# The chunk recurrence of a hybrid decoder: four moves in the order of three engines' work

## The reference, cut to what matters

```
mLSTM (4 heads, 64 x 64):
  mt  = max(b + m, max over s<=t of (b_t - b_s + li_s));  w_inter = exp(b + m - mt)
  qk  = (q k^T) * exp(draw - mt)           num = w_inter * (q C) + qk v;  den likewise with n
  h   = num / max(|den|, exp(-mt))         C = w_c * C + ks^T v   (ks = k * exp(...))
gated DeltaNet (4 heads, 128 x 128):
  a   = strictly lower(beta * (k k^T) * gam);   solve (a + I) [w_v, w_k] = [v*beta, k*beta*exp(d)]
  u   = w_v - w_k S;   o = (q*exp(d)) S + ((q k^T)*gam) u;   S = exp(dl)*S + kdec^T u
HGRN2 (4 heads, 64 x 64):
  attn_ts = sum over channels of q_tc k_sc exp(bc_tc - bc_sc)
  o   = (q*exp(bc)) S + attn i;            S = exp(bl) * S + (k*exp(bl-bc))^T i
```

## Time and profile before

| | |
|---|---|
| median of 3 runs | 1974.97 us (1974.41 to 1976.78) |
| profiled execution | 1972.25 us, with a span of 1970.5 us |
| TensorE, share of the span | 1763.4 us, 89% |
| DVE, ACT, POOL | 913.5, 830.7 and 98.1 us |
| recurrence, first layer | 262 to 448 us, TensorE busy 149.03 us, mean granted clock 0.92 |
| recurrence, second layer | 1224 to 1406 us, TensorE busy 147.55 us, mean granted clock 0.94 |

### The profile page before, as it was taken

One profiled execution on the slowest core, in us unless ns is written; L12 is line 12 of the kernel. 1 busy time (PEld: TensorE's weight loads), 2 busy tenths in 40 slices (PEclk: granted clock), 3 DMA queues, 4 the chain that ended last, 5 costly groups with the idle time before them and its releaser, 6 DMA issues. The chain is left out here.

```text
span 1970.5 us, 35425 instructions
## 1 busy us (share of the span) xinstructions
PE 1763.4 (89%) x13446; PEld 1681.1 (85%) x13446; DVE 913.5 (46%) x1960; ACT 830.7 (42%) x1860; POOL 98.1 (5%) x165
## 2 busy tenths in 40 slices
PE   5999968878879999999889998788688799999995
PEld 5999957775679999999879997687658799999995
DVE  5275257756552222244363823666662522223354
ACT  5235555655243333333242355455542433333332
POOL 0020110003000000000002011000300000000000
PEclk8999999986789999999989999999669899999997
DMA  5322000003653323322042210000329223323211
GB/s 171 90 81 68 9 5 1 1 1 74 131 106 98 88 85 86 105 81 75 2 146 80 82 44 4 1 1 1 71 71 142 80 85 86 90 85 112 72 35 46
DMA packets 128706, 132.80 MB, mean 67 GB/s; under 512 B 32630, under 2 KB 95522, under 8 KB 128584
## 3 DMA queue, kind: packets, MB, share of 16 engines
q1 hardware_dynamic: 128584, 131.22, 25.1%
HBM read 121.53 MB, written 9.66 MB: 67 GB/s over the span
## 5 line engine op out<-in xcount | busy, mean ns | idle before, releaser
L307 PE MATMUL bank<-arena 128*128 128x272 f32 (+4 forms) x3488 | 1013.7, 291 | 32.2 <-DVE arena L414 14.7
L309 PE MATMUL bank<-arena 128*128 128x272 f32 (+4 forms) x3488 | 1011.0, 290 | 0.0
L308 PE MATMUL bank<-arena 128*128 128x272 f32 (+4 forms) x3488 | 1006.4, 289 | 0.0
L307 PEld LDWEIGHTS bank<-arena 128*128 128x128 f32 (+1 forms) x3488 | 655.2, 188 | 39.2 <-issue 25.3
L308 PEld LDWEIGHTS bank<-arena 128*128 128x128 f32 (+1 forms) x3488 | 656.2, 188 | 3.0 <-issue 2.1
L309 PEld LDWEIGHTS bank<-arena 128*128 128x128 f32 (+1 forms) x3488 | 655.8, 188 | 0.9
L351 DVE TENSOR_TENSOR arena<-sbuf,arena 128x512 fp32r<-128x512 f32 x296 | 201.2, 689 | 350.2 <-ACT arena L347 350.0
L347 ACT CAST arena<-sbuf 128x512 fp32r<-128x512 f32 x296 | 180.6, 622 | 352.2 <-PE bank L309 304.0
L2943 DVE TENSOR_TENSOR arena<-sbuf,arena 128x544 fp32r<-128x544 f32 x88 | 63.8, 724 | 143.2 <-ACT arena L2887 143.2
L2887 ACT CAST arena<-sbuf 128x544 fp32r<-128x544 f32 x88 | 56.9, 647 | 163.2 <-PE bank L309 160.0
L347 ACT CAST arena<-arena 128x512 fp32r<-128x512 f32 (+1 forms) x128 | 77.7, 622 | 112.7 <-PE bank L309 104.4
(11 more groups left out here) (374 smaller groups left out, 1794.0 us busy)
## 6 DMA issues: line engine op xcount, KB each, us to landing
sbuf<-in_w_gate_up SPq DMA_DIRECT2D x176, 256.0 KB, 3.1
arena<-in_w_in SPq DMA_DIRECT2D x96, 256.0 KB, 2.8
sbuf<-in_w_down SPq DMA_DIRECT2D x88, 256.0 KB, 2.6
arena<-in_w_in SPq DMA_DIRECT2D x32, 260.0 KB, 2.6
sbuf<-in_w_out SPq DMA_DIRECT2D x32, 256.0 KB, 4.8
sbuf<-in_state_gdn_S SPq DMA_DIRECT2D x8, 512.0 KB, 6.2
out_s_S<-sbuf SPq DMA_DIRECT2D x8, 512.0 KB
arena<-in_x_prompt SPq DMA_DIRECT2D x4, 512.0 KB, 7.4
```

What stands on the lines that cost most here:

```text
L307: pe.matmul(out, wH, hH, start=first, stop=False)
L308: pe.matmul(out, wH, hL, start=False, stop=False)
L309: return pe.matmul(out, wL, hH, start=False, stop=last)
```

## The change

Only the order changes; each operation and each wait is the same, and every semaphore has the same counts, except that the four exponentials get a wait of their own.

- TensorE: `mix_turn(b - 1)` goes ahead of `hg_diagonal(c)` and `inverse_start(c)` (in round 4, which has neither, its place is the same).
- TensorE: at a round's end, `hg_scores(c, 5)` and `key_products(c + 1)` go ahead of `ml_key_turn(b)`, which now stands right before `ml_delta(b)`.
- ACT: the four exponentials become `ml_rises(b)`, behind `inverse(c, 3)` and `first_product(c, 3)`.
- DVE: the addition that makes `m_next` goes from the end of `ml_differences` to `ml_decayed`, behind `ml_scores`; in rounds with a `now` part `hg_place(c, 0)`, `hg_operands(c, 2)` and `update(c, 3)` lie between as well.
- DVE: `hg_place(c, 4)` and `hg_operands(c, 6)` go ahead of `update(c, 6)`, and so ahead of `ml_outputs(b)`.

```diff
@@ TensorE
                 if old:
                     kS(b)
+                if i > 1:
+                    mix_turn(b - 1)
                 if now:
                     hg_diagonal(c)
                     inverse_start(c)
-                if i > 1:
-                    mix_turn(b - 1)
...
-                if old:
-                    ml_key_turn(b)
-                if now:
                     hg_scores(c, 5)
                     if c + 1 < CHUNKS:
                         key_products(c + 1)
                 if old:
+                    ml_key_turn(b)
                     ml_delta(b)
@@ ACT
                 act.activation(mW, mW, ACT.Exp).then_inc(sig["E"], 1)
+
+            def ml_rises(c):
+                act.wait_ge(*done("mW", c))
...
                     first_product(c, 3)
+                if old:
+                    ml_rises(b)
+                if now:
                     weighted_values(c)
@@ DVE
-                dve.wait_ge(*done("wexp", c))
-                tt(mp.rearrange("p h b -> p (h b)"), cols[:, 1, c, 0:4], M[:, :, T - 1], ALU.add
-                   ).then_inc(sig["m_next"], 1)
...
                     dve.wait_ge(*done("num", c - 1))
+                tt(mp.rearrange("p h b -> p (h b)"), cols[:, 1, c, 0:4], M[:, :, T - 1], ALU.add
+                   ).then_inc(sig["m_next"], 1)
                 mul(mqw, m.mlF[:, 0:2, at(c)], wexp).then_inc(sig["mqw"], 1)
...
                 if now:
+                    hg_place(c, 4)
+                    hg_operands(c, 6)
                     update(c, 6)
                 if old:
                     ml_outputs(b)
-                if now:
-                    hg_place(c, 4)
-                    hg_operands(c, 6)
```

## The result

The changed kernel took 1941.91 us in the median of 4 runs (1939.66 to 1951.77), the kernel before 1974.69 on the same chip. The ratio of the two is on record as 0.9852, 95% interval 0.9828 to 0.9875, which is some 29 us; the two medians, of four runs each, lie 32.8 us apart. The profiled execution took 1942.64 us (span 1940.9), 29.6 less than the one before.

What follows compares the result with a forecast made beforehand. The prediction took TensorE's idle time, some 36 us in each of two recurrences, as what could be won; 12.6 + 6.1 + 1.9 + 2.0 = 22.6 us, clock -3.0 and +1.5, net 21 off 1974.97: 1954 us, range 1946 to 1965.

Steps and rivals of the forecast that it cites:

- A: Level 3's `inverse_second`, three rounds per layer: TensorE idles 1.88 us for copies queued behind four exponentials; moving these gives 9.4 us.
- C: Round 4: DVE's addition waits 2.19 us for the exponentials, ahead of the scores product; moving it gives 3.2 us.
- B: Round ends: key turning waits 1.89 us for `ml_outputs`, delaying key products; 6.1 us over four boundaries (rounds 1-2, 2-3).
- all three new waits: At a round boundary, TensorE would newly wait before the delta product (0.7 us), `mix_turn` (1.5) and `hg_diagonal` (0.7).
- The clock: TensorE's clock in the recurrences: -3.0 for boundaries falling to 1.2 GHz, +1.5 for one low stretch removed, 21 us net.
- the way from round 3 to 4: Boundary without key products or `hg_diagonal`: `mix_turn` starts earlier, about 1.0 us a layer, 2.0 in all.
- The -3.0: Half of the four boundaries (rounds 1 to 2, 2 to 3) assumed to fall to 1.2 GHz, costing 3.0 us.
- The +1.5: One stretch at 1.2 GHz after round 3's wait for the inverse copies, assumed to regain full clock: 1.5 us.
- third rival: Idle time gathered before `hg_diagonal` costs more clock than the waits cost: slower, 1985 us; chance 0.04.
- The sum of 22.6: Gain of the reordering in the recurrences before clock effects: 12.6 + 6.1 + 1.9 + 2.0 us.
- two starts: Boundary from round 0 to 1, one per layer: the 0.95 us wait for `hg_place` 4 goes, 1.9 us.
- Rival 2: Recurrences: everything pays and no boundary falls to 1.2 GHz, 26 us gained, 1949 us; chance 0.08.

Runs made afterwards that it cites:

- again: The changed kernel measured once more, with no further edit: 1940.02 us, ratio 0.9855 to the kernel before.
- fill: Kernel before, order unchanged, with 12 useless turnings before level 3's `inverse_second` and 12 before the key turning: 1953.25 us, ratio 0.9917.
- before2: The kernel before, unchanged, profiled a second time: its two recurrences take 364.7 us together, against 362.9 in the first profile.
- keys: Kernel before with only the key products ahead of the key turning, and `hg_place` 4 and `hg_operands` 6 ahead of `update` 6: 1967.16 us, ratio 0.9995.
- rises: Kernel before with only the four exponentials moved behind the copies and the addition behind the scores: 1951.55 us, ratio 0.9923.
- nomix: Changed kernel with `mix_turn` back behind `hg_diagonal` and `inverse_start`: 1942.5 us, ratio 0.9857 to the kernel before.
- keys_fill: Kernel with only the key products moved, plus 12 useless turnings before level 3's `inverse_second` and 20 before `hg_diagonal`: 1950.68 us, ratio 0.991.
- nomix_fill: Changed kernel with `mix_turn` back behind `inverse_start` and 8 useless turnings in the wait before `hg_diagonal`: 1941.89 us, ratio 0.9854.
- norises: Changed kernel with the four exponentials and the addition back in their old places: 1962.1 us, ratio 0.9966 to the kernel before.

## Why the prediction was wrong

What it said of the order of work came out at almost every place: A (0.18 us left of 1.88), C (max columns 0.30), B (8.67 us for 8.74 in three of the four long boundaries, 9.5 in the one that falls; the key products 0.05 after `update` 6), all three new waits (0.51, 1.38, 0.48 for 0.7, 1.5, 0.7). *The step that failed is "The clock"*: "I let half of the four long boundaries fall to 1.2 GHz, -3.0, and give back the one stretch behind A, +1.5". The clock brought 8 to 12 us where this step has -1.5, and two terms of the sum, B's boundaries and the way from round 3 to 4, were too large because they held a part of it.

- *The -3.0.* It took the clock in the boundaries as full before and as something to lose. All four were low already, and in the changed kernel one is (376.90 above; 12.51 against 11.67, 0.84 us), in again none.
- *The +1.5.* I had read one low stretch, and there were more. Before's order at the full clock can be estimated from fill: 356.05 us, less 2 x 1.63 for its own falls at the end (12.12 against 10.49), makes 352.8. Before took 362.9, so it lost 10.1 us to the clock: 4.3 in the long boundaries, 1.6 in round 3, 4.2 from round 3 to the end. The slow key products of the earlier trace rows and the slow turnings of the earlier trace rows were such places; I read the turnings as evidence for the third rival, and neither as a loss of before. And I took a stretch as full as the first of the earlier trace rows to have the full clock: the second is as full, 3.40 of 3.40 us, and has 0.50. The changed kernel loses 1.7 in its profiled execution and nothing in again; before2 lost 11.9. So the clock brought 8.4 to 11.9 us instead of -1.5.
- *The sum of 22.6.* At the full clock on both sides the order is worth 352.8 - 335.5 = 17.3: six A at 1.69 instead of 1.57, 10.1 for 9.4; four boundaries at 0.61, 2.4 for 6.1; two starts at 0.83, 1.7 for 1.9; C with round 3 to 4 3.1 for 5.2. The two mis-sized terms were measured between marks that held low stretches: the forecast's 2.05 and 1.02 a boundary start from distances of 10.8 and 9.8 us to `inverse_first` 1, which are 9.3 in fill. With the clock inside, as I had read them, the terms give 11.2, 5.9, 1.7 and 6.9, which is the 25.7. That 22.6 comes near it is partly luck: the order was too large by 5.3 and the clock too small by 9.9.
- *The base.* 12.1 us lie between 1954 and 1941.9: 4.6 in the recurrences (25.7 for 21.1), 3.9 outside, 2.7 because I took the gain off the median and not off the profiled execution, and 0.7 by which the profiled execution of the changed kernel lies above its median; the rest is rounding. The 4.6 alone would have left the time at 1949, inside the range. But between before2 and again the recurrences differ by 364.7 - 335.5 = 29.2 us, 17.3 of order and 11.9 of clock, and that is the whole gain by the ratios.
- *The rivals.* Rival 2 (the clock stays up) named half of the mechanism, and I gave it 0.08 and 26 us; that the boundaries were low before isn't in it, and 25.7 beside its 26 is luck too, for its order is 24.6 and the measured one 17.3. Rival 3's mechanism is real, as keys shows, though keys isn't slower than before. What I missed is that the edits aren't independent: A's pause can bring down the clock behind it, and B's worth hangs on that. Alone, keys' gain can't be told from nothing; with A mended, the step from rises to nomix is 0.9923 - 0.9857, 0.66% of the time.
- `mix_turn`, costed at nothing, is nothing by itself. In the whole it takes 0.46 us from a boundary that doesn't fall (12.13 to 11.67), three quarters of what the order gives there: the forecast's 8.74 us had no turnings behind `hg_diagonal`, and with them there it is 9.15 (keys_fill). In the traced execution of nomix one of two boundaries falls; that `mix_turn` ahead prevents it isn't shown, for one falls in the changed kernel too.

The Trainium skill ("TensorE: Matmul & The Clock Gate", Part 1: The HAM clock gate) says that activity releases the throttle, and names no condition that the work be useful; fill and keys_fill agree, at some 16 and 17 us, while in nomix_fill the filler didn't keep one boundary of each layer from falling. In its section "HAM oscillation — how this bites in real kernels" it describes a kernel that falls anew with every tile; norises, which falls in each of the three rounds that have A, agrees in this, though the pause here is 1.88 us and the waits there are of 3 to 5 us for DMA. The size of a fall here, 1.63 us, is from norises.

## What to carry to other kernels

Take the stretches at 1.2 GHz out of the trace first and sum the gain of an order against a kernel, or a stretch of it, held at the full clock; then state the clock's share as a term of its own, scanning the whole region slice by slice and not the one stretch that caught the eye. Where TensorE idles for a microsecond or two in each round, mend the pause that the clock falls behind, or try a dozen useless turnings in it, before judging other edits: until then they may show no gain. Check in the trace that the clock held, for useless work doesn't always do it (nomix_fill). Don't add up parts that were timed alone.

## What the runs showed of the hardware

- In norises TensorE was granted 1.00 while it stood still for 1.88 us, and fell to 1.2 GHz 0.5 to 1.2 us after it was at work again, in all six places (the first: 311.60 to 318.00); one such fall cost 1.63 us of a round. In rises the clock fell in the pause itself, 0.4 us before the key turning at 332.37.
- Pauses of the same length at the same place fall in one execution and not in another: before's round 3 took 29.14 us in one layer and 27.52 in the other, and before2 the reverse (27.51, 29.15).
- Twelve turnings that compute nothing, about 1.5 us in a pause of 1.88, were enough in fill to hold the full clock behind each such pause, for a ratio of 0.9917 (0.9893 to 0.9942). Eight, 1.1 us in a pause of 2.95, were not in one long boundary of each layer (nomix_fill).
